# Handed-over first loads, shared gate banks, a later start of tile 5's dots and fewer stores, in an encoder layer with retrieved experts

## The reference, cut to what matters

```python
def encoder_layer(x, ...):
    xn = rmsnorm(x, norm1_g)
    a, hy, gates = split(xn @ w_in)              # widths 512, 3 * 512, 2 * 1024
    ya = multiscale_pool(a, ...) @ w_pool_out
    yb = hyena_mixer(hy, ...) @ w_hyena_out      # short conv, long conv by FFT, products
    h = x + (sigmoid(gate_a) * ya + sigmoid(gate_b) * yb) @ w_o
    return h + peer(rmsnorm(h, norm2_g), peer_wq, peer_keys, peer_u, peer_v)

def peer_block(xb, wq, keys, u_tab, v_tab):      # blocks of 128 tokens
    q = (xb @ wq).reshape(T, 8, 2, 128)
    s = einsum('thpc,hpkc->thpk', q, keys)       # 2 x 128 scores per head
    sv, si = top_k(s, 16)                        # then the best 16 of the 16 x 16 sums
    ...                                          # idx: 128 experts per token; gate: softmax
    act = gelu(einsum('ted,td->te', u_tab[idx], xb)) * gate
    return einsum('te,ted->td', act, v_tab[idx])
```

## Time and profile before

| | us |
|---|---|
| median of 3 runs | 3261.31 (3257.53 to 3262.63) |
| the profiled execution | 3266.24 |
| its span | 3264.6 |
| PE busy | 2897.8 (89%) |
| DVE busy | 1682.5 (52%) |
| POOL busy | 1559.7 (48%) |
| ACT busy | 556.9 (17%) |
| moved by DMA | 1004.39 MB, mean 308 GB/s |

### The profile page before, as it was taken

How to read it: one execution, slowest core, us unless ns; L and a number is a source line. 1 busy time by engine, 2 the same in 40 slices (tenths; PEclk the granted TensorE clock), 3 DMA queues, 4 the chain that set the end, 5 groups by cost and what they waited for, 6 DMA issues and landing times.

```text
span 3264.6 us, 29062 instructions
## 1 busy us (share of the span) xinstructions
PE 2897.8 (89%) x10143; PEld 1451.7 (44%) x10143; DVE 1682.5 (52%) x3842; ACT 556.9 (17%) x1190; POOL 1559.7 (48%) x1335
## 2 busy tenths in 40 slices
PE   5999989667789979846699999999999999999996
PEld 3656648323334445423344444444444444443331
DVE  4341126797997645787355564455654444441101
ACT  3211123000115455545100000000000000000000
POOL 2211113256674635527556566556555555653343
PEclk9999989878999989977799999999999999999998
DMA  3332263698899999879999999999999999998786
GB/s 132 119 100 71 90 214 115 218 332 295 295 374 355 356 364 361 296 271 354 397 370 377 394 376 372 391 391 393 373 380 386 371 381 383 372 390 290 278 290 235
DMA packets 343064, 1004.39 MB, mean 308 GB/s; under 512 B 31143, under 2 KB 113831, under 8 KB 340360
## 3 DMA queue, kind: packets, MB, share of 16 engines
q0 software_dynamic: 184320, 671.17, 54.4%
q1 hardware_dynamic: 156872, 306.21, 26.5%
q10 hardware_dynamic: 1728, 25.17, 1.9%
HBM read 950.26 MB, written 52.17 MB: 307 GB/s over the span
## 4 chain that ended last, share of the span: by engine, by line
PE 59%; DMA 10%; DVE 7%; ACT 3%; POOL 2%; issue 2%; SPq 0%; DVEq 0%; ACTq 0%; POOLq 0%
PE job_ps L1485 20%; PE wide_ps L1469 20%; PE v_ps L1506 9%; PE wide_ps L610 4%; DMA v_rows<-in_peer_v,row_t 4%; PE job_ps L610 3%; DMA tmp_gates<-arena 2%; DVE u_row L1718 2%; DMA u_row<-in_peer_u,row_u 2%; PE gate_ps L1457 2%; POOL u_row L1393 2%; ACT arena L1579 1%; ACT arena L1571 1%; DMA arena<-tmp_gates 1%; DMA arena<-in_inv_cnt 1%
## 5 line engine op out<-in xcount | busy, mean ns | idle before, releaser
L1403 POOL DMA_INDIRECT v_rows<-in_peer_v,row_t x640 | 690.4, 1079 | 761.0 <-PE v_ps L1506 584.2
L1393 POOL DMA_INDIRECT u_row<-in_peer_u,row_u x640 | 746.4, 1166 | 429.5 <-DVE dots L1718 203.9
L1718 DVE CUSTOM_DVE_ANT_0 u_row<-u_row,x_tile 128x1024 f32<-128x1024 f32 x640 | 771.1, 1219 | 93.6 <-DMA u_row<-in_peer_u,row_u 90.6
L1469 PE MATMUL wide_ps<-arena 128*128 128x384 f32 x2048 | 689.0, 490 | 0.0
L1485 PE MATMUL job_ps<-arena 128*128 128x512 f32 x1536 | 687.6, 596 | 0.0
L1469 PEld LDWEIGHTS wide_ps<-arena 128*128 128x128 f32 x2048 | 385.5, 191 | 322.8 <-issue 84.8
L1485 PEld LDWEIGHTS job_ps<-arena 128*128 128x128 f32 x1536 | 287.5, 190 | 370.0 <-issue 341.0
L1506 PE MATMUL v_ps<-v_rows,diag 128*32 128x512 f32 x2560 | 373.0, 619 | 82.1 <-DMA v_rows<-in_peer_v,row_t 81.9
L1756 DVE TENSOR_TENSOR arena<-arena,job_ps 128x512 f32<-128x512 f32 x192 | 131.8, 686 | 483.5 <-PE job_ps L1485 483.0
L874 POOL TENSOR_TENSOR exact<-arena,exact 128x1024 fp32r<-128x1024 f32 x48 | 118.1, 2463 | 445.4 <-ACT exact L622 445.4
L1607 ACT ACTIVATE arena<-wide_ps 128x384 f32<-128x384 f32 x128 | 62.9, 491 | 1483.9 <-PE wide_ps L1469 1483.9
(11 more groups left out here) (242 smaller groups left out, 2240.6 us busy)
## 6 DMA issues: line engine op xcount, KB each, us to landing
arena<-in_peer_ut SPq DMA_DIRECT2D x128, 512.0 KB, 9.1
arena<-in_peer_v SPq DMA_DIRECT2D x128, 512.0 KB, 9.0
arena<-in_w_in SPq DMA_DIRECT2D x64, 512.0 KB, 6.2
tmp_gates<-arena ACTq DMA_DIRECT2D x12, 2048.0 KB, 10.3
arena<-tmp_gates SPq DMA_DIRECT2D x32, 768.0 KB, 21.3
arena<-in_w_o SPq DMA_DIRECT2D x32, 512.0 KB, 5.8
arena<-in_wq SPq DMA_DIRECT2D x32, 512.0 KB, 4.6
u_row<-in_peer_u,row_u POOLq DMA_INDIRECT x640, 8.9
```

The costliest lines, as they stand in the source:

```text
L1393: pool.indirect_dma_start(u_row[n % NU][:], None, dram["peer_u"], bass.IndirectOffsetOnAxis(row_u[g % 2][:, e:e + 1], 0)).then_inc(u_in[n ...
L1403: pool.indirect_dma_start(v_row[n % NV], None, dram["peer_v"], bass.IndirectOffsetOnAxis(row_t[g % 3][:, t:t + 1], 0)).then_inc(v_in[n % N ...
L1469: last = pe.matmul(wide[j % 2][:, 0:TD], uw[j % NW][:, k * P:(k + 1) * P], x_t[:, k], start=k == 0, stop=k == KD - 1)
L1718: dve.tensor_tensor_reduce(out=u_row[n % NU][:], in0=u_row[n % NU][:], in1=xb[g % 2][:], scale=1.0, scalar=0.0, op0=ALU.mult, op1=ALU.add, ...
```

## The change

1. A class `Handed` keeps 28 KB per partition and seven semaphores over both parts. After `t2` 7 of the first part SP issues the loads that the second part begins with: xn1 (four of 512 KB) and three weights of 512 KB. The first part's filter taps, DFT columns, `y` and `zt` use that room before, and its arena has 90 KB instead of 118 KB.
2. In the second part the bank `gate_ps` joins the four banks of the units. The early gate halves are guests in the rotation: `share` gives each job and each guest, in queue order, the bank whose last use is longest past, but not one that holds open `r` sums. Both halves of an early chunk are multiplied at +2 and evicted at +3, and ACT evicts ahead of that beat's unit work. Chunks 16 to 31 come at beats 203 to 248. The late chunks stay.
3. Row 256 is fetched and multiplied at beat 270 instead of 256, and rows go on at four in three beats until row 309 is back at its own beat. `chosen(5)` starts at beat 256 at two steps a beat; rankings and gates of tiles 4 and 5 move by a few beats.
4. xn2 is stored for gathered tiles alone, and the scores of the last two tiles of a sequence alone (tiles 2, 3 and 6, 7).

```diff
+class Handed:
+    def __init__(self, m):
+        self.hand = m.sb("hand", [P, 28 * KB])
+        self.xn, self.w_raw = cut(self.hand, 0, KD, L), [cut(self.hand, (16 + 4 * r) * KB, D) for r in range(3)]
+        self.x_in, self.landed = [m.sem(f"next_x{t}") for t in range(LT)], [m.sem(f"next_w{r}") for r in range(3)]
...
-        self.bank_of, self.before, last = [], [], {}
-        for job, (kind, n, u) in enumerate(self.owner):
-            b = job % len(banks)
-            self.bank_of.append(b)
-            self.before.append(last.get(b))
-            last[b] = job
...
+    def share(self, order):
+        self.bank_of, self.before, self.guest, taken = [], [], {}, []
+        last = [(-1, None, None)] * len(self.banks)
+        for at, (reader, guest, held) in enumerate(order):
+            bank = min((b for b in range(len(self.banks)) if last[b][2] not in held), key=lambda b: (last[b][0], b))
+            if guest is None:
+                self.bank_of.append(bank)
+                self.before.append(last[bank][1])
+            else:
+                self.guest[guest] = bank, last[bank][1]
+            last[bank] = at, reader, len(self.bank_of) - 1 if guest is None else None
...
-                sp.dma_start(d["xn2"][:, at:at + D], self.normed[tt % 2]).then_inc(self.n_out[tt % 2], 16)
+                if tt in self.stored:
+                    sp.dma_start(d["xn2"][:, at:at + D], self.normed[tt % 2]).then_inc(self.n_out[tt % 2], 16)
...
-                sp.dma_start(d["scores"][self.seq * LT:(self.seq + 1) * LT, n // 2].rearrange("n p k -> p n k"),
+                sp.dma_start(d["scores"][self.seq * LT + 2:(self.seq + 1) * LT, n // 2].rearrange("n p k -> p n k"),
...
+    def first_loads(self, sp):
+        d = self.dram
+        for tt in range(LT):
+            sp.dma_start(self.next.xn[:, :, tt * P:(tt + 1) * P],
+                         d["xn1"][:, tt].rearrange("p (k q) -> p k q", k=KD)).then_inc(self.next.x_in[tt], 16)
+        for r, tile in enumerate((X1_T, V_T, X1_T + 1)):
+            sp.dma_start(self.next.w_raw[r], d["w_in"][tile]).then_inc(self.next.landed[r], 16)
...
+                if unit == ("t2", 2 * LT - 1):
+                    sp.wait_ge(p.y_added, CT)
+                    sp.wait_ge(p.next_out, 16)
+                    p.first_loads(sp)
...
-    CHOSEN = {1: (40, 1), 4: (LAST + 1, 4), 5: (LAST + 7, 10)}
-    RANKED_AT = (2, 51, 149, 187, LAST + 3, LAST + 10, LAST + 124, 494)
-    GATED_AT = (8, 58, 152, 191, LAST + 6, LAST + 14, LAST + 130, 502)
+    CHOSEN = {1: (40, 1), 4: (LAST + 1, 4), 5: (LAST + 8, 2)}
+    RANKED_AT = (2, 51, 149, 187, LAST + 4, LAST + 13, LAST + 124, 494)
+    GATED_AT = (8, 58, 152, 191, LAST + 6, LAST + 20, LAST + 130, 502)
+    GAP = 14
+    DOT_AT = [n if n < 2 * P else max(n, 2 * P + GAP + 3 * (n - 2 * P) // 4) for n in range(ROWS)]
...
-    CHUNK_AT += [CHUNK_AT[-1] + 6 + 3 * c for c in range(EARLY // 2)]
+    CHUNK_AT += [CHUNK_AT[-1] + 3 + 3 * c for c in range(EARLY // 2)]
...
-        p = Pre(m, dram, "p1", 1, (), units, [wide[0], wide[1], job_ps[0], job_ps[1]], 3, small)
+        p = Pre(m, dram, "p1", 1, (), units, [wide[0], wide[1], job_ps[0], job_ps[1], gate_ps], 3, small, handed)
...
+                if kind == "r" and i % KD in (0, KD - 1):
+                    held = () if i % KD else tuple(jobs)
...
+                if n == CHUNK_AT[c] + 2:
+                    order += [((evicted, 2 * c + u + 1), (c, u), held) for u in range(2)]
...
-                if n < ROWS:
-                    fetch_u(n)
+                for r in range(ROWS):
+                    if DOT_AT[r] == n:
+                        fetch_u(r)
...
-                    if c or u:
-                        pe.wait_ge(evicted, 2 * c + u)
+                    pe.wait_ge(*p.guest[c, u][1])
...
-                        if n == CHUNK_AT[c] + (2 + 2 * u if c < EARLY else 2):
+                        if n == CHUNK_AT[c] + 2:
                             gates(c, u)
...
             for n in range(END):
+                for c in range(EARLY):
+                    if n == CHUNK_AT[c] + 3:
+                        for u in range(2):
+                            evict(c, u)
                 pre.upto(tick_of(n, LAG, ROWS) * US)
```

More of the change, by code:

```diff
@@ L277, with __init__ @@
             "o": 5.6, "r": 2.8, "t2": 0.6, "q": 5.6, "s": 1.4}
-    def __init__(self, m, dram, tag, seq, split, units, banks, ring, small):
+    def __init__(self, m, dram, tag, seq, split, units, banks, ring, small, given=None):
         self.dram, self.tag, self.seq, self.split, self.units = dram, tag, seq, split, units
@@ L390, in free @@
         if before is not None:
-            pe.wait_ge(*self.read_by(before))
+            pe.wait_ge(*before)
     def sync(self, sp):
         d, R = self.dram, self.ring
[L397 to L401, removed]
+        if not self.given:
+            for tt in range(LT):
                 sp.dma_start(self.x[:, tt], d["x"][self.seq][:, tt]).then_inc(self.x_in[tt], 16)
-        if not self.ready:
             sp.dma_start(self.gain, d["norm1_g"].broadcast_to([P, D])).then_inc(self.gain_in, 16)
-        for wi in range(R):
-            self.load_weight(sp, wi)
+            for wi in range(R):
+                self.load_weight(sp, wi)
         ci = 0
@@ L471, in drain @@
         for b in range(2):
-            sp.wait_ge(self.n_out[b], 16 * 2)
+            sp.wait_ge(self.n_out[b], 16 * sum(t % 2 == b for t in self.stored))
             sp.wait_ge(self.s_out[b], 16 * (H // 2))
@@ L877, with __init__ @@
 class Filters:
[L880 removed]
+    def __init__(self, m, dram, arena, at, spread, cols, banks):
         self.dram, self.cols, self.banks = dram, cols, banks
@@ L1282, in second_and_experts, with gate_bank @@
             "added", "ms", "root", "inv", "normed", "stored", "cleared", "pre_gone"))
+        order, unit, held = [], 0, ()
+        for n in range(CHUNK_AT[EARLY]):
+            while unit < len(units) and p.begin[units[unit]] <= tick_of(n, LAG, ROWS) * US:
+                kind, i = units[unit]
+                jobs = [job for job, owner in enumerate(p.owner) if owner[:2] == (kind, i)]
+                order += [(p.read_by(job), None, ()) for job in jobs]
+                if kind == "r" and i % KD in (0, KD - 1):
+                    held = () if i % KD else tuple(jobs)
+                unit += 1
+            for c in range(EARLY):
+                if n == CHUNK_AT[c] + 2:
+                    order += [((evicted, 2 * c + u + 1), (c, u), held) for u in range(2)]
+        assert unit == len(units)
+        p.share(order)
+        def gate_bank(c, u):
+            return p.banks[p.guest[c, u][0]] if c < EARLY else (gate_ps, wide[0])[u]
         block = ctx.enter_context(nc.Block())
@@ L1337, in _ @@
                     for b in range(2):
-                        sp.wait_ge(p.n_out[b], 32)
+                        sp.wait_ge(p.n_out[b], 16 * sum(t % 2 == b for t in p.stored))
                     load_x(2)
@@ L1847, in _ @@
                     js += 1
-                if n < ROWS:
-                    dot(n)
+                for row in range(ROWS):
+                    if DOT_AT[row] == n:
+                        dot(row)
                 route_on(n, 1)
```

112 lines of the change are left out of this document (54 added, 58 removed).

## The result

The median fell from 3259.42 to 3233.66 us (four runs each): a ratio of 0.9911, 95% interval 0.989 to 0.9931, so 22 to 36 us less. Run again beside its variants, the same kernel had a median of 3225.22 (five runs, 3215.69 to 3231.59) and a ratio of 0.9884 (0.9866 to 0.9902). Forecast were 3221 and 40 us less, with 3205 to 3238 as the forecast's own range; both levels lie in it. The first level is 26 us under the kernel before, the second 38 us under the kernel before as measured beside it (3263.44).

The account below looks back on a forecast made before the run. PE was taken to bound the dense stretch, with DMA beside it, and DVE, DMA or PE the stretches before. Terms -2 + 3 - 22 - 18 - 9 + 9 - 1 = -40 us took the median from 3261.3 to 3221, range 3205 to 3238.

Parts of the forecast that it names:

- The burst in the first part: First part's end: query weight 4 waits behind seven handed loads, PE 3.4 us late; +3 us, bounds 0 and 9.6.
- Less traffic beside the first gathers: Start of second part: up to two weights' bytes move into the idle time before it; -2 us, bounds 0 and -3.4.
- Part 2: Units' stretch, 900 to 1405: PE's eviction waits shrink from 36.4 to 14 us, ACT's store wait nearly goes; -22 us.
- Rival 3: Units' stretch: shared banks tie PE to ACT, early halves each stop PE 1.7 us; slower, 3315 us; chance 0.12.
- Part 3, the hole: After tile 4's gates: POOL goes straight to v rows, next quad 16 to 19 us earlier; -18 us, bounds 0 and -27.
- Part 3, bytes: 8 fewer u rows by beat 285 save 9 us, fetching them in beats 285 to 309 costs 9; sum nothing.
- Part 4: Second part: 2.6 MB fewer stores, PE the nearer limit; -1 us, bounds 0 and -7.5.
- The dense stretch: Dense experts, 1624 to 2926 us: bound by PE, slides as a block, same length; over 5 us longer refutes the prediction.
- Rival 1: Units' stretch, 900 to 1405: bytes bind, parts 2 and 4 give only 7.5 us; 3237 us; chance 0.18.
- Rival 2: Late chunks: DVE's chain keeps the hole, part 3 is worth 0; 3239 us; chance 0.14.

Follow-up runs that it names:

- loads spread: Kernel after, with the seven handed loads issued one at a time behind query units 2 to 13 of the first part, not as one burst: 3217.42 us, ratio 0.9863.
- one gate bank, old beats: Kernel after with part 2 undone: one bank for all early gate halves, four for the units, earlier beats and ACT order: 3258.3 us, ratio 0.9997.
- the base: Another name for the loads spread variant of the kernel after: 3217.42 us, ratio 0.9863.
- the gap of 28: Loads spread variant with the gap doubled, row 256 at beat 284 and four rows in three beats until row 368: 3225.73 us, ratio 0.9897.
- no-gap runs: Part 3 undone, row 256 back at beat 256: on the kernel after 3233.54 us, ratio 0.9917; on the loads spread variant 3226.36 us, ratio 0.9897.
- start loads: Kernel after, with the seven first loads of the second part issued by SP at that part's start, not behind t2 of the first: 3218.74 us, ratio 0.9871.

## Why the prediction was right, point by point

**The burst in the first part: forecast +3, measured +7.0 to row 0 (+7.6 in the second profile), about half of it given back.** The place was right: PE waits at the second score unit. In the kernel after:

```profile
479.25 12.12 SPq L503 DMA_DIRECT2D hand<-tmp_xn  x4
494.39 5.97 SPq L497 DMA_DIRECT2D arena<-in_wq  x3
502.03 1.06 ACT L647 ACTIVATE exact<-arena 128x1024 fp32r<-128x1024 f32 x1 [13.19 <-DMA arena<-in_wq]
503.63 2.08 PE L622 MATMUL pre_ps<-arena 128*128 128x128 f32 x8 [3.63 <-ACT arena L735]
```

I had let query weight 4 be issued at 487.90 as in the earlier trace rows; SP reached it at 494.39, since the four strided loads kept it for 12.12 us and the three weights until 494.35. Once issued it took 7.6 us to land instead of 3.7. The split came 10.4 us later than before, where I had added 9.6, and PE's next step 4.1 us later, where I had 3.4: both nearly right. In the second profile the seven handed loads and weight 4 land in the order of their issue, weight 4 last at 502.71 after 501.43: it did come behind the whole burst, as the +3 in place of 0 had assumed.

What the term left out is the clock. At the next score unit PE is 7.1 us late and not 4.1 (512.92 for 505.85), and it stays so to the part's end. These are ten microseconds of PE around its wait, before and then after:

```profile
500.00:510.00 10.00, 10.00 (x52) 8.49 (x52) 5.27 (x34) 2.94 (x5) 3.66 (x2) 1.00 0.48 157
```
```profile
500.00:510.00 10.00, 6.37 (x20) 5.41 (x21) 3.04 (x21) 4.90 (x7) 6.83 (x3) 0.66 0.39 142
```

The granted clock, 1.00 there before, is 0.50 (1.2 GHz, the lower of the two levels) from the end of PE's wait of 3.6 us to about 509.6: 6 us of work at half speed, so 3 us on top of the wait. With the loads spread it stayed at 1.00.

**Less traffic beside the first gathers: forecast -2.** Not shown. The six profiles with the burst have row 0 at 626.7 in the mean and row 134 at 902.9, the seven variants without it 620.0 and 899.3: of 6.7 us about 3 are given back. The kernel with spread loads hands over the same bytes and takes 280.0 us from row 0 to row 134, as before (279.4); after takes 274.5. What varies is a wait on DVE for the pool branch's constants, in before from 603 to 900, then in after from 603 to 902:

```profile
DVE arena L862 <- DMA arena<-in_inv_cnt: 12.4, 3, 8.4
```
```profile
DVE arena L887 <- DMA arena<-in_inv_cnt: 8.8, 3, 7.1
```

Over all fourteen profiles the stretch goes with this wait nearly one for one: 273 to 275 us where it is 6 to 9 us, 279 to 282 where it is 12 to 14. But one burst kernel (one gate bank, old beats) has the full wait, 13.6 us, and row 134 at 907.3. So a late start falls into this slack in some executions and not in others; no run held that wait fixed.

**Part 2: forecast -22, measured -22.4 in the second profile (497.5 to 475.1), -12.5 in the first.** The mechanism was half right. (These are before against after; against the variant with all but part 2 it is -21.) I had put the gain on the bank and the store's timing as two causes that add. The runs show that each alone is worth -7 or does harm (+22), and that only both give -22. The waits fell further than forecast for evictions (36.4 to 4.9, not 14), and for the store to 19 and 23, not under 15. Rival 3 did not come: with shared banks PE hardly waits for evictions, and the one kernel slower than before shares none.

The term stopped too early. By the medians part 2 is worth 33 us, not 22 (3258.3 without it, 3225.22 with it; 37 by the ratios), and the base without part 3 is 34 us under the kernel before. The rest lies mostly behind row 250, where I had given part 2 nothing. From row 250 to the last job the kernel before takes 1808.2 us; part 3 without part 2 takes 14.0 off it, part 2 without part 3 12.3 or 14.6, both together 22 (30 on the base). With part 2 the last early chunk is evicted 19 us after row 250, not 60. Why this shortens the way from there to the dense part is not shown.

**Part 3, the hole: forecast -18, measured -22** from chunk 31 to chunk 32 (59.5 to 37.7 on the spread base). I had the next quad some 6 us behind the turn; its v rows landed while PE stood for tile 4's gates, so it followed at once.

**Part 3, bytes: forecast -9 and then +9.** This step failed in its first half. The late chunks did not get shorter (79.6 to 80.4 us), as the gap of 28 explains. The second half came as +6.6 from the last eviction to the product (18.6 to 25.2). The two misses, 4 too little and 9 too much, leave part 3 at -15.3 by the marks and -9 by the medians (3226.36 to 3217.42; -11 by the ratios), where -18 was forecast.

**Part 4: forecast -1.** Measured 2.4 us of medians, not told apart from nothing.

**The dense stretch** kept its length: from first product to last job 1619.2 and 1622.6 us, before 1620.3.

**The total.** From before to the second profile of after the marks give +1.5 us up to row 134, -22.4 from there to row 250 and -21.6 from there to the last job, where the terms of the sum had +1, -23 and -18. That the level came so near is in part luck: part 2 gave some 11 us more than its term, the burst cost 4 more, and part 3 gave 7 to 9 less.

Rival 1 (bytes bind in the units' stretch) fell: the stretch shortened to 474 us at a DMA share of 0.96. Rival 2 fell with the no-gap runs. Open is why after is 7 to 8 us above the variants that don't burst while row 134 differs by 3.6 us in the mean; after's two profiles take 1786 us from row 250 to the last job, the spread and start loads 1778 and 1781, but variants with no burst also took 1785 and 1788. The intervals of the ratios overlap.

## What to carry to other kernels

A wait on a shared buffer that has two causes, the buffer itself and what its reader stands behind, was here worth its time only when both went; undo them one at a time before pricing them as a sum, and follow each past the stretch in which it waits. When a stall is taken out of a stretch, ask which chain is next there and how long it is: two limits of 80 us look like one until one is taken down. And a burst of early loads costs its issuing queue too, and a short wait that it brings PE can cost a few microseconds more at the lower clock, so put it where that queue has time, one load at a time.

## What the runs showed of the hardware that was not expected

Four loads of 512 KB with 512-byte pieces on the SBUF side kept SP for 12.12 us when they stood behind 4 MB of stores and loads, and for 4.36 us on an idle DMA (loads at start, 603.86). A wait of 3.6 us between dense matmuls (after, 500 to 503.6) was followed by some 6 us at a granted clock of 0.50 (0.57 over 502 to 510), where the kernel before ran at 1.00. Executions of one kernel spread by 16 us (after again, five: 3215.69 to 3231.59) and 17 us (before beside it, twelve: 3252.91 to 3269.83), and two profiles of after differ by 10 us over 116 beats of the same instructions.
